# Squares added up on VectorE, a single-pass forget bias, and 64-column levels of a recurrence, in a two-block transformer kernel

## What is computed

```python
x = x + 0.5 * swiglu(rmsnorm(x, g1))             # ffn1, width 2816
x = x + mix(rmsnorm(x, g2)) @ w_out              # mixing
x = x + 0.5 * swiglu(rmsnorm(x, g3))             # ffn2
rmsnorm(x, g) = x * rsqrt(mean(x * x) + 1e-6) * g
# mixing, from one projection w_in:
#   forgetting attention, 4 heads: q.k/8 + c[t] - c[s], c = cumsum(log sigmoid(f + bias))
#   dilated attention, 4 heads, with a partial rotation
#   gated linear recurrence (HGRN), 4 heads of 128 x 128 states
```

## Time and profile before

| | |
|---|---|
| median of 3 runs | 2554.13 us (2541.73 to 2555.55) |
| profiled execution, own time | 2549.08 us |
| span of the profiled execution | 2547.3 us |
| PE busy over the span | 2301.9 us (90%) |
| DVE, ACT busy | 1096.2 us (43%), 713.5 us (28%) |
| HBM read | 624.33 MB, mean 246 GB/s |
| the second block begins | at about 1390 us of the span |

### The profile page before, as it was taken

How to read it: one execution, slowest core, us unless ns; L and a number is a source line. 1 busy time by engine, 2 the same in 40 slices (tenths; PEclk the granted TensorE clock), 3 DMA queues, 4 the chain that set the end, 5 groups by cost and what they waited for, 6 DMA issues and landing times. The chain is left out here.

```text
span 2547.3 us, 36442 instructions
## 1 busy us (share of the span) xinstructions
PE 2301.9 (90%) x15022; PEld 1671.9 (66%) x15022; DVE 1096.2 (43%) x1679; ACT 713.5 (28%) x912; POOL 34.8 (1%) x31
## 2 busy tenths in 40 slices
PE   6966767999999999999998799998999999998998
PEld 4635765443333333333333799987999999988998
DVE  4546444121111221111112565675656665676654
ACT  3332113110000010010001543534433433535332
POOL 0001100000000000000000000000000000000000
PEclk8967888999999999999999899999999999999999
DMA  9630025899999999999997465532565555433551
GB/s 371 235 151 1 1 67 213 359 416 417 417 417 417 417 416 417 418 417 417 417 408 269 150 199 181 160 110 69 192 193 171 182 182 182 149 100 118 180 182 66
DMA packets 236111, 626.84 MB, mean 246 GB/s; under 512 B 13132, under 2 KB 153964, under 8 KB 200044
## 3 DMA queue, kind: packets, MB, share of 16 engines
q1 hardware_dynamic: 232796, 622.35, 65.0%
q10 hardware_dynamic: 3216, 3.06, 0.4%
HBM read 624.33 MB, written 1.05 MB: 246 GB/s over the span
## 5 line engine op out<-in xcount | busy, mean ns | idle before, releaser
L1837 DVE TENSOR_TENSOR w_low<-ring,w_high 128x2048 fp32r<-128x2048 f32 x168 | 384.0, 2290 | 308.8 <-ACT w_high L1832 308.7
L1832 ACT ACTIVATE w_high<-ring 128x2048 fp32r<-128x2048 f32 x168 | 320.2, 1909 | 276.6 <-PE bank L2030 138.2
L1594 PE MATMUL bank<-ring,ut 128*64 128x512 f32 x1024 | 256.6, 655 | 59.5 <-DMA ring<-in_exp_w_dram 59.3
L1565 PE MATMUL bank<-ring,xt 128*64 128x512 f32 x1024 | 223.3, 594 | 0.3 <-ACT xt L1648 0.3
L1565 PE MATMUL bank<-ring_odd,xt 128*64 128x512 f32 x1024 | 223.3, 594 | 0.0
L1594 PEld LDWEIGHTS bank<-ring,ut 128*64 128x64 f32 x1024 | 74.6, 149 | 225.9 <-issue 130.3
L2045 PE MATMUL bank<-h_high,w_high 128*128 128x256 f32 x1408 | 186.8, 281 | 15.2 <-ACT h_high L1930 15.2
L2045 PEld LDWEIGHTS bank<-h_high,w_high 128*128 128x128 f32 x1408 | 175.5, 189 | 16.0 <-ACT h_high L1930 15.8
L2045 PE MATMUL bank<-h_high,w_low 128*128 128x256 f32 x1408 | 185.6, 280 | 0.0
L2045 PE MATMUL bank<-h_low,w_high 128*128 128x256 f32 x1408 | 185.5, 280 | 0.0
L2045 PEld LDWEIGHTS bank<-h_high,w_low 128*128 128x128 f32 x1408 | 175.1, 189 | 0.0
(11 more groups left out here) (519 smaller groups left out, 3060.3 us busy)
## 6 DMA issues: line engine op xcount, KB each, us to landing
ring<-in_exp_w_dram SPq DMA_DIRECT2D x256, 1024.0 KB, 22.5
ring_odd<-in_exp_w_dram SPq DMA_DIRECT2D x128, 1024.0 KB, 21.6
ring<-in_ffn_w_gate_dram SPq DMA_DIRECT2D x44, 1024.0 KB, 5.4
ring<-in_ffn_w_up_dram SPq DMA_DIRECT2D x44, 1024.0 KB, 5.4
ring<-in_ffn_w_down_dram SPq DMA_DIRECT2D x44, 1024.0 KB, 4.9
ring<-in_w_in_dram SPq DMA_DIRECT2D x36, 1024.0 KB, 5.5
ring<-in_ada_w_dram SPq DMA_DIRECT2D x24, 1024.0 KB, 12.4
ring<-in_w_out_dram SPq DMA_DIRECT2D x8, 1024.0 KB, 5.1
```

The costliest lines, as they stand in the source:

```text
L1565: ins = nc.tensor.matmul(bank[b][at:at + SLOTS, :], xt[:, c, SLOTS * side:SLOTS * side + SLOTS], (ring, ring_odd)[side][:, c, 512 * q:512 ...
L1594: ins = nc.tensor.matmul(bank[2 + dh][64 * dh:64 * dh + 64, :], ut[:, r % 4, 64 * (r // 4):64 * (r // 4) + 64], w[:, x, 512 * dh:512 * dh ...
L1832: nc.scalar.activation(w_bufs[0][u % BUFS], ring2[:, u % RING2, :], ACT.Copy).then_inc(high2, 1)
L1837: nc.vector.tensor_tensor(w_bufs[1][u % BUFS], ring2[:, u % RING2, :], w_bufs[0][u % BUFS].bitcast(F32), ALU.subtract).then_inc(low2, 1)
```

## The change

1. `add_squares`, on DVE behind the split of unit u+2, adds the eight chunks of squares down to one in three adds (4, 2 and 1 chunks of 256), each waiting for the one before; `add_up` on PE is then one matmul. All six phases use it.
2. The forget term is computed on 36 rows in place of 4: rows 0 to 3 and, again, 32 to 35. `fox_parts` holds its rounded value in the first four and the rest in the others, as `F32R`, and one picking matrix (`pick_fox`) adds both in a single pass. `fox_bias`, `ff_parts` and `w_ff`'s copies are laid out twice; the constant parts are written in `tables`.
3. Levels 1 to 7 multiply only the 64 query columns that the level's mask can select. The eight products fill one bank (6 or 7 by turns), and one `copy_predicated` of 128 x 8 x 64 takes them. Level 0 keeps its size, with two copies of 128 x 512 in place of four. Level n of PE waits for the factors and for the copies of level n-2 (level 1 for both of level 0); `cross` waits for those of level 6 and not of level 7. `at_` now covers all of `hT`, four blocks a head, of which `on_diagonal` is cleared by POOL.

```diff
             def add_up(pe):
-                for c in range(DC):
-                    if c % 2 == 0:
-                        pe.wait_ge(sem(f + "squares"), c // 2 + 1)
-                    ins = nc.tensor.matmul(total, ones, squares[:, c, :], start=(c == 0), stop=(c == DC - 1))
-                ins.then_inc(sem(f + "total"), 1)
+                pe.wait_ge(sem(f + "squares_added"), 3)
+                nc.tensor.matmul(total, ones, squares[:, 0, :], start=True, stop=True).then_inc(sem(f + "total"), 1)
+
+            def add_squares(dve):
+                dve.wait_ge(sem(f + "squares"), 4)
+                for i, n in enumerate((4, 2, 1)):
+                    if i:
+                        dve.wait_ge(sem(f + "squares_added"), i)
+                    nc.vector.tensor_tensor(squares[:, 0:n, :], squares[:, 0:n, :], squares[:, n:2 * n, :], ALU.add
+                                            ).then_inc(sem(f + "squares_added"), 1)
...
-                            ins = nc.tensor.matmul(b, pick_head[:, h, :], fox_c[:, 0:KEYS[a]], start=False, stop=True)
+                            ins = nc.tensor.matmul(b, pick_fox[:, h, :], fox_parts[:, 0:KEYS[a]], start=False, stop=True)
...
-                    for h in range(4):
-                        if n and h % 2 == 0:
-                            pe.wait_ge(sem(f + "masked_in"), 2 * (n - 1) + h // 2 + 1)
...
+                    else:
+                        pe.wait_ge(sem(f + "masked_in"), max(2, n))
+                        for h in range(4):
+                            for a in range(TT):
+                                at = P // 2 * (2 * h + a)
+                                later = qp[:, h, P * a:P * a + P].rearrange("p (k two b) -> p k two b", two=2, b=2 ** (n - 1))[:, :, 1, :]
+                                ins = nc.tensor.matmul(bk[6 + n % 2][:, at:at + P // 2], kr[:, h, P * a:P * a + P], later, start=True, stop=True)
+                        ins.then_inc(sem(f + "level_ready"), 1)
 
                 def cross():
                     pe.wait_ge(sem(f + "factors"), NLEV)
-                    pe.wait_ge(sem(f + "masked_in"), 2 * NLEV)
+                    pe.wait_ge(sem(f + "masked_in"), NLEV)
...
-                    st.tell(nc.vector.tensor_scalar(fox_c[0:4, :], fz[:, 1, :], -8.0, None, ALU.mult), f + "fox_ready")
+                    st.step(nc.vector.tensor_scalar(fz[:, 0, :], fz[:, 1, :], -8.0, None, ALU.mult))
+                    st.step(nc.vector.tensor_copy(fox_parts[0:FOX_ROWS, :], fz[:, 0, :]))
+                    st.tell(nc.vector.tensor_tensor(fox_parts[32:36, :], fz[32:36, 0, :], fox_parts[32:36, :].bitcast(F32), ALU.subtract), f + "fox_ready")
...
+                    if n == 0:
+                        for j in range(2):
+                            st.tell(nc.vector.copy_predicated(on_diagonal[:, 4 * j:4 * j + 4, :], level_masks[:, 0:P].unsqueeze(1).to_broadcast([P, 4, P]),
+                                                              bk[6 + j][:, :].rearrange("p (c t) -> p c t", c=4)), f + "masked_in")
+                    else:
+                        b = 2 ** (n - 1)
+                        at = P + P // 2 * (n - 1)
+                        mask = level_masks[:, at:at + P // 2].rearrange("p (k b) -> p k b", b=b).unsqueeze(1).to_broadcast([P, DC, P // (2 * b), b])
+                        later = on_diagonal.rearrange("p c (k two b) -> p c k two b", two=2, b=b)[:, :, :, 1, :]
+                        st.tell(nc.vector.copy_predicated(later, mask, bk[6 + n % 2][:, :].rearrange("p (c k b) -> p c k b", c=DC, b=b)), f + "masked_in")
...
-                st.step(nc.vector.tensor_copy(ff_parts[0][:, :, :], w_ff[:, :, :]))
-                st.tell(nc.vector.tensor_tensor(ff_parts[1][:, :, :], w_ff[:, :, :], ff_parts[0][:, :, :].bitcast(F32), ALU.subtract), f + "ff_low")
+                for at in (0, 32):
+                    ins = nc.vector.tensor_copy(ff_parts[0][:, :, at:at + 4], w_ff[:, :, :])
+                st.step(ins)
+                for at in (0, 32):
+                    ins = nc.vector.tensor_tensor(ff_parts[1][:, :, at:at + 4], w_ff[:, :, :], ff_parts[0][:, :, at:at + 4].bitcast(F32), ALU.subtract)
+                st.tell(ins, f + "ff_low")
...
                     split_low(dve, base_unit + n + AHEAD)
+                    if n == 0:
+                        add_squares(dve)
...
-                nc.vector.tensor_copy(flat(level_masks[:, :, :]), levels)
+                nc.vector.tensor_copy(level_masks[:, :], levels)
+                nc.vector.tensor_copy(pick_fox[:, :, :], const("pick_head").rearrange("p (h t) -> p h t", h=4))
+                nc.vector.tensor_scalar(fox_parts[:, :], const("pick_head")[:, 0:T], 0.0, None, ALU.mult)
+                for part in ff_parts:
+                    ins = nc.vector.tensor_scalar(part[:, :, :], const("ones")[:, 0:DC].unsqueeze(2).to_broadcast([P, DC, FOX_ROWS]), 0.0, None, ALU.mult)
+                st.step(ins)
```

More of the change, by code:

```diff
@@ L140, in shape_constants @@
     for b in (1, 2, 4, 8, 16, 32, 64):
-        levels.append((i[:, None] // (2 * b) == i[None] // (2 * b)) & (i[None] % (2 * b) >= b) & (i[:, None] % (2 * b) < b))
+        later = i[i % (2 * b) >= b]
+        levels.append((i[:, None] // (2 * b) == later[None] // (2 * b)) & (i[:, None] % (2 * b) < b))
     return base, rwkv, np.concatenate(levels, 1).astype(np.float32)
@@ L1776, in build @@
         prods = sb("prods", [P, 4 * T])
-        levels = prods[:, 0:NLEV * P]
+        levels = prods[:, 0:LEVEL_COLS]
         rope2 = sb("rope2", [P, 2, T])
         lower = sb("lower", [P, 2, 4])
-        fox_bias = sb("fox_bias", [4, LAYERS])
-        level_masks = sb("level_masks", [P, NLEV, P], U8)
+        fox_bias = sb("fox_bias", [FOX_ROWS, LAYERS])
+        level_masks = sb("level_masks", [P, LEVEL_COLS], U8)
         U_MIX = FFN_UNITS
@@ L1870, in _ @@
                 st = Steps(dve, sem, "dve_step")
+                st.tell(nc.vector.memset(fox_bias[:, :], 0.0), "bias_cleared")
                 for m in range(DC):
@@ L1901, in build @@
         w_ff = sb("w_ff", [P, DC, 4])
-        ff_parts = [sb(f"ff_{part}", [P, DC, 4], F32R) for part in ("high", "low")]
+        ff_parts = [sb(f"ff_{part}", [P, DC, FOX_ROWS], F32R) for part in ("high", "low")]
         one_less = sb("one_less", [P, 4])
@@ L1909, in build @@
         o_hgrn = fgt
-        at_ = hT[:, 2:8, :].rearrange("p c t -> p (c t)").rearrange("p (h b t) -> p h b t", h=4, b=3)
-        fz = masked[0:4, :, :].rearrange("p b n -> p (b n)").rearrange("p (r t) -> p r t", t=T)
+        at_ = hT[:, :, :].rearrange("p c t -> p (c t)").rearrange("p (h b t) -> p h b t", h=4, b=4)
+        on_diagonal = hT[:, :, :].rearrange("p c (two t) -> p c two t", two=2)[:, :, 0, :]
+        fz = masked[0:FOX_ROWS, :, :].rearrange("p b n -> p (b n)").rearrange("p (r t) -> p r t", t=T)
         hgrn_parts = [sb(f"hgrn_{part}", [P, 4, T], F32R) for part in ("high", "low")]
@@ L2162, in mixing @@
             sem = S.sem
[L2163 removed]
+            parts_high, parts_low, add_squares, add_up, take_root, turn_root, first_unit = phase(
                 S, f, lambda c: ("mix_norm_2", L * DC + c), False, flip)
[L2165 removed]
             bk = [bank[i ^ flip] for i in range(8)]
@@ L2218, in forget @@
                         for c in range(DC):
-                            ins = nc.tensor.matmul(bk[5][0:4, 0:T], w[:, c, :], h[:, c, :], start=(k == 0 and c == 0), stop=(k == 2 and c == DC - 1))
+                            ins = nc.tensor.matmul(bk[5][0:FOX_ROWS, 0:T], w[:, c, :], h[:, c, :], start=(k == 0 and c == 0), stop=(k == 2 and c == DC - 1))
                     ins.then_inc(sem(f + "ff_ready"), 1)
@@ L2503, in forget_logits @@
                     dve.wait_ge(sem(f + "ff_ready"), 1)
-                    st.step(nc.vector.tensor_tensor(fz[:, 0, :], bk[5][0:4, 0:T], root[0:4, :], ALU.mult))
+                    st.step(nc.vector.tensor_tensor(fz[:, 0, :], bk[5][0:FOX_ROWS, 0:T], root[0:FOX_ROWS, :], ALU.mult))
                     st.step(nc.vector.tensor_scalar(fz[:, 0, :], fz[:, 0, :], fox_bias[:, L:L + 1], None, ALU.add))
@@ L2565, in level @@
                         st.step(nc.vector.tensor_tensor(k4[:, :, 0, :], k4[:, :, 0, :], halves[:, :, 1:2].to_broadcast([P, blocks, b]), ALU.mult), f + "factors")
[L2566 to L2571, removed]
+                    if n == 0:
+                        for j in range(2):
[7 more added lines that the diff above has]
+                        st.tell(nc.vector.copy_predicated(later, mask, bk[6 + n % 2][:, :].rearrange("p (c k b) -> p c k b", c=DC, b=b)), f + "masked_in")
                 def take_cross():
-                    dve.wait_ge(sem(f + "level_ready"), 2 * NLEV + 1)
-                    dve.wait_ge(sem(f + "masked_in"), 2 * NLEV)
+                    dve.wait_ge(sem(f + "level_ready"), NLEV + 2)
+                    dve.wait_ge(sem(f + "masked_in"), NLEV + 1)
```

36 lines of the change are left out of this document (22 added, 14 removed).

## The result

The changed kernel takes 2564.72 us (median of 19 runs, 2551.95 to 2572.63), the kernel before 2552.62 (also of 19), 12 us apart: **a ratio of 1.0065, 95% interval 1.0049 to 1.0081**, which is 13 to 21 us slower. The forecast was 2547 us with a range up to 2558: wrong in sign. The profiled execution took 2572.63 us (its span is 2570.8).

The account below looks back on a forecast made before the run. PE was taken as the bound (busy 90%). Squares -8.8, first ffn's tables +0.95, two mixings -2.9 and clock falls +6 made -4.7 us, from 2551.6 to 2547 us; range 2535 to 2558.

Parts of the forecast that it names:

- Squares on PE, -8.8 us: Seven of eight square-sum matmuls go, 2.93 us a phase; kept in three ffn phases, with DVE's adds (2.47 us) hidden.
- First ffn: Layer 0's first ffn: no gain, +0.95 us from longer tables, and PE idle 4.7 us before unit 7.
- Mixing, handed on to level 1, +1.5 us and an idle of 4.4: Each mixing: PE starts level 1 1.5 us later, after some 4.4 us idle in place of 1.6.
- Masked copies, 0.70 us: Mixing levels on DVE: one copy of 0.70 us replaces four of 1.44; -0.4 at `mix_low(0)`, -0.74 behind level 7.
- The rival of dear copies: Masked copies on short runs could cost several times 0.70 us; at 3 us each, +11, 2563 us; chance 0.05.
- Forget term, 0.4 a head: Mixing scores: a single pass saves 0.4 us a head, between 0.2 and 0.7; four heads, -1.6 us a layer.
- Levels on PE, nothing: Mixing levels on PE: half the columns do not make the products faster; no gain counted.
- The rival of larger savings: 64-column levels take half (-5), or the forget term saves 0.7 a head; 2536 us without clock falls; chance 0.15.
- The clock, three falls at 2 us, +6: Granted clock halves behind three longer pauses: unit 7 of the first ffn and level 1 of both mixings; 2 us each.
- My slow rival: Clock costs more than saved: 3.3 us at each of three stretches, 3 more at layer 1's turn 5; 2554 us; chance 0.2.

Follow-up runs that it names:

- e7: The changed kernel with the masks' tile kept at 1024 bytes a partition, of which 576 are used; ratio 1.0033 to the kernel before.
- e13: e7 with the tables computed in three pieces and the mixing's pauses filled with unread products; ratio 0.9959 to the kernel before.
- e3: The kernel before with only the levels of 64 columns, one bank and one masked copy (two for level 0); ratio 1.0077 to the kernel before.
- e6: The kernel before with an unused tile of 576 bytes a partition behind the masks and nothing else; ratio 1.0036 to the kernel before.
- e12: The kernel before with 512 unused bytes behind the masks; one execution, 1110.8 us from first square sum to last output copy, against 1109.0 before.
- e10: The kernel before with 32 unused bytes behind the masks; one execution, 1125.6 us from first square sum to last output copy, against 1109.0 before.
- e11: The kernel before with 96 unused bytes behind the masks; one execution, 1115.5 us from first square sum to last output copy, against 1109.0 before.
- e9: The kernel before with squares added on DVE, tables in three pieces and four pauses of each mixing filled with unread products; ratio 0.9962 to the kernel before.
- e14: e3 with the masks' tile kept at 1024 bytes and unread products filling three pauses of each mixing; ratio 0.9975 to the kernel before.

## Why the prediction was wrong

The sum was -8.8 + 0.95 - 2.9 + 6. Two steps of it failed: the last term, the clock, had three new falls where nine came and was too small, and a term was missing, the pace of products that the change leaves alone. The masked copies of two levels saved less than I took. The waits and hand-overs behind the other terms were right.

- **Squares on PE, -8.8 us**: right. The square sum and the next unit start 0.24 us apart (1644.85, 1645.09), the adds took 2.40 us, and the three ffn phases of e7, at the old pace, are 2.7, 2.6 and 2.0 us shorter. In the changed kernel the slower pace takes 1.5 us of each of these phases back (1.7 and 1.4 in the table; the last phase, 190.7 against 192.0, does not show it).
- **First ffn**: the pause was right: at the old pace, in e7, it is 4.6 us against 4.7, and 4.1 in the changed kernel, whose slower products ahead of it fill the rest. The price was not: +6.6 us in all, of which e7 at the old pace has 4.0, with half clock from 1477 to 1483.6, and the pace the others. The clock cost some 3 us here where I took 2.
- **Mixing, handed on to level 1, +1.5 us and an idle of 4.4**: right to 0.1 us in the changed kernel (4.35); at the old pace, in e7, the idle is 4.6.
- **Masked copies, 0.70 us**: right from level 3 on (0.71), and for level 0 (0.66). Levels 1 and 2, whose runs are 1 and 2 elements, take 1.32 and 1.30 us. The rival of dear copies had the mechanism and not the size: 1.44 is what four copies took before, so nothing is lost, but 0.6 us of gain at each of four places is not there.
- **Forget term, 0.4 a head**: at head 0 the scores and their terms fill 1.52 us (1686.41 to 1687.93) in place of 2.00: 0.48. The 36 rows cost nothing: the scaling of 36x256 took 0.28 us (changed, 1669.57), as that of 4x256 before.
- **Levels on PE, nothing**: right, 1.89 us for the 16 loads of level 2, two for each of its eight products. The rival of larger savings is out.
- **The clock, three falls at 2 us, +6**: this step failed. The traces show the clock as a share of the full one; its GHz no run shows. All three came, with 20 us at half clock together. But at six places more the clock fell where it had not before, for 31 us together: at level 3 of layer 0, with no wait over 0.6 us ahead of it; in both layers at the unit that waits for the values to be taken (1.5 us, as before) and behind `values(6)`, whose pauses were 3.2 and 3.0 us before and are 3.2 and 3.1 now; and at turn 5 in layer 1. That makes 48 us more at half clock than before, not the 20 at most of three stretches. Its price can be read from e7 to e13, in one trace each: 6.6 and 7.3 us a mixing (with a little from shorter pauses), where I took 2. My slow rival had the mechanism and turn 5 of layer 1, and stopped at 9.9 + 3.
- **Not in the sum at all: the slower pace, 118.7 and 120.0 ns for 117.8, +10 us.** The diff has the line, `level_masks` at `[P, LEVEL_COLS]`; I read it as a smaller cast. With the tile at its old size (e7) the pace is 117.8 ns again and the ratio is 1.0033 (1.0012 to 1.0054), still slower than before: the clock and the copies were enough to turn the sign.

The two failures add up in the profiled executions: -4.7 and 10 for the pace make +5.3 of the measured +14.2, and the 8.9 left over and the 6 counted make 15 us lost in 48 more at half clock, where 24 would be the most. How they are shared out between the clock and the copies that saved less is not settled. Nor is what made the levels alone (e3) as slow as the whole; its interval reaches down to 1.0049.

## What to carry to other kernels

When a change resizes or adds a tile, matmuls that it leaves alone can change their pace (an unused tile of 576 bytes took them from 117.8 to 118.7 ns, e6): compare the start-to-start time of an untouched matmul, phase by phase, before any reasoning on the change, and pad the tile to its old size as the first experiment. Where PE is the bound in one stage and waits in the next, work taken from it ahead of a wait is no gain but a longer pause, and here longer pauses were charged again in clock (0.50 in the windows of 6.6 and 5.6 us at the end of those of 4.1 and 4.35 us), also at other places; fill them with products into an unused bank, or move what is late, and time both.

## What the runs showed of the hardware

- Rounded products of 128 x 256 ran at full granted clock at 117.8 ns before and in every kernel whose masks kept their 1024 bytes with nothing unused behind them, and with 512 unused bytes (e12); at 120.0 with 32 (e10); at 118.7 with 576 (e6) and with masks of 576 bytes (changed, e3), where one ffn of each of the three ran at 120.0; with 96 (e11) at 117.3 in two ffn phases and at 120.0 in the two others. Why is open.
- In the changed kernel a masked copy of 512 columns from PSUM took 0.70 to 0.74 us in runs of 4 elements and more, and 1.30 to 1.32 in runs of 1 and 2. The product on runs of 1 that the levels do on VectorE was not slower: 0.70 us for 512 columns at level 1, 0.68 to 0.69 at the levels behind. Why only the copy was slower is open.
- Stretches at half clock behind 1440 us lasted 3 to 10 us, and one began at 1698.8 us with no wait over 0.6 us in the 10 us before (changed kernel). With pauses filled there were two of them between 1440 and 2500 us (e9, e13 and e14, 6.8 us each).
